# Second FFN up projection, rounds 4 to 11: both units as block products, with weight sums added up in DRAM during the first mixer

## The reference, cut to what matters

```python
h = rms_norm_2(x, ffn_norm_g[l]) * (1 + scale_f) + shift_f
u, v = jnp.split(h @ w_up[l], 2, axis=-1)          # w_up: 1024 x 5632, u and v 2816 columns each
u = causal_depthwise_conv(u, conv_w[l], conv_b[l])
x = x + gate_f * ((jax.nn.silu(u) * v) @ w_down[l])
```

## Time and profile before

| | us |
|---|---|
| runs | 1345.43, 1350.05, 1346.85 |
| median | 1346.85 |
| profiled execution | 1345.38 |
| its span | 1343.4 |
| PE busy | 1331.0 |
| DVE / ACT / POOL busy | 857.3 / 624.0 / 658.7 |
| bytes moved by DMA | 150.59 MB |

### The profile page before, as it was taken

The page is one execution under the profiler, slowest core; times in us unless marked ns, Lnnn a source line. Parts: engine busy times, 40 slices in busy tenths (PEclk is TensorE's granted clock), DMA queues, the critical chain, the costliest instruction groups (busy, mean ns, idle before and its releaser), DMA issues.

```text
span 1343.4 us, 21993 instructions
## 1 busy us (share of the span) xinstructions
PE 1331.0 (99%) x8268; PEld 1135.0 (84%) x8268; DVE 857.3 (64%) x1682; ACT 624.0 (46%) x1097; POOL 658.7 (49%) x369
## 2 busy tenths in 40 slices
PE   8999999999999999999999999999999999999998
PEld 7878888888998888888889976788998999988887
DVE  5898876456778676767897879724579454431222
ACT  7236566564364445453222525675344454542222
POOL 7555232126254444445553489733364776654441
PEclk9999999999999999999999999999999999999999
DMA  7931121115525444444673241121242223252221
GB/s 218 227 102 41 56 63 49 30 35 172 173 87 180 141 142 147 152 149 141 202 228 107 77 112 48 50 64 48 79 157 94 93 96 115 75 201 97 86 87 63
DMA packets 188903, 150.59 MB, mean 112 GB/s; under 512 B 21625, under 2 KB 186723, under 8 KB 188304
## 3 DMA queue, kind: packets, MB, share of 16 engines
q1 hardware_dynamic: 187104, 148.78, 35.8%
q10 hardware_dynamic: 1200, 0.36, 0.1%
q0 software_dynamic: 512, 0.25, 0.1%
HBM read 145.18 MB, written 4.19 MB: 111 GB/s over the span
## 4 chain that ended last, share of the span: by engine, by line
PE 93%; DVE 4%; ACT 1%; issue 1%; POOL 0%; DMA 0%; DVEq 0%; ACTq 0%
PE ps L2638 28%; PE ps L2639 27%; PE ps L2640 27%; PE ps L2832 2%; PE ps L2888 1%; PE ps L2917 1%; DVE qd L2291 1%; DVE hf L2299 1%; PE ps L3120 1%; PE ps L3164 0%; PE ps L3149 0%; PE ps L2722 0%; PE ps L3093 0%; PE ps L3186 0%; DVE hs L2334 0%
## 5 line engine op out<-in xcount | busy, mean ns | idle before, releaser
L914 POOL TENSOR_TENSOR w_lo<-raw,w_hi 128x1024 fp32r<-128x1024 f32 (+2 forms) x210 | 487.2, 2324 | 569.2 <-ACT w_hi L1021 436.0
L2638 PE MATMUL ps<-h_hi,w_hi 128*128 128x512 f32 (+1 forms) x1308 | 478.4, 366 | 0.1
L2639 PE MATMUL ps<-h_lo,w_hi 128*128 128x512 f32 (+1 forms) x1308 | 474.1, 362 | 0.0
L2640 PE MATMUL ps<-h_hi,w_lo 128*128 128x512 f32 (+1 forms) x1308 | 473.5, 362 | 0.0
L2638 PEld LDWEIGHTS ps<-h_hi,w_hi 128*128 128x128 f32 x1308 | 247.2, 189 | 41.9 <-issue 5.0
L2640 PEld LDWEIGHTS ps<-h_hi,w_lo 128*128 128x128 f32 x1308 | 247.1, 189 | 38.7
L1021 ACT ACTIVATE w_hi<-raw 128x1024 fp32r<-128x1024 f32 (+2 forms) x166 | 164.7, 995 | 244.4 <-PE ps L2640 222.9
L2639 PEld LDWEIGHTS ps<-h_lo,w_hi 128*128 128x128 f32 x1308 | 247.4, 189 | 35.6
L2638 PE MATMUL ps<-g_hi,w_hi 128*128 128x512 f32 (+1 forms) x394 | 144.9, 368 | 0.0
L2640 PE MATMUL ps<-g_hi,w_lo 128*128 128x512 f32 (+1 forms) x394 | 144.4, 366 | 0.0
L2639 PE MATMUL ps<-g_lo,w_hi 128*128 128x512 f32 (+1 forms) x394 | 144.3, 366 | 0.0
(11 more groups left out here) (408 smaller groups left out, 1999.2 us busy)
## 6 DMA issues: line engine op xcount, KB each, us to landing
ada<-in_ada_w SPq DMA_DIRECT2D x48, 512.0 KB, 3.7
raw<-in_ffn_w_up SPq DMA_DIRECT2D x22, 1024.0 KB, 4.9
raw<-in_w_up SPq DMA_DIRECT2D x22, 1024.0 KB, 4.9
raw<-in_w_in SPq DMA_DIRECT2D x21, 1024.0 KB, 5.1
raw<-in_ffn_w_down SPq DMA_DIRECT2D x8, 896.0 KB, 5.9
raw<-in_w_down SPq DMA_DIRECT2D x8, 896.0 KB, 5.0
raw<-in_w_in SPq DMA_DIRECT2D x16, 256.0 KB, 3.7
raw<-in_w_out SPq DMA_DIRECT2D x4, 1024.0 KB, 5.1
```

The lines of the kernel that those rows point to most:

```text
L914: pool.tensor_tensor(w_lo[slot % 4][:, 0:nk, :], part[:, :, slot % 2 * P:(slot % 2 + 1) * P], w_hi[slot % 4][:, 0:nk, :].bitcast(F32), ALU ...
L2638: pe.matmul(out_ap, w, x, start=first, stop=False, **kw)
L2639: pe.matmul(out_ap, w, xl, start=False, stop=False, **kw)
L2640: return pe.matmul(out_ap, wl, x, start=False, stop=last, **kw)
```

## The change

**All of rounds 4 to 11 as block products.** `R1` goes from 10 to 11, and both u and v pairs are made in seven products: 16 pairs, numbered p, 112 products in one sequence `PRODUCTS`. For pair p, PE now runs (p,6) (p,2) (p+1,1) (p,7) (p,3) (p+1,5) (p,4); no plain tile stands between. Two sets of four PSUM banks alternate between pairs.

**Work moved between engines.** `w_add` on DVE is gone. Instead DVE makes the low parts of products 2, 3 and 4 (`product_low`), POOL those of 1, 5, 6 and 7. ACT rounds all seven. The second tile of a pair now comes out negated, which the taps and `gated_up` take back.

**Weight sums come from DRAM.** Four tensors `kept_sums1` to `4`, each of shape `[2, 512, 8, 128]` (4 MB), hold the four sums of weight blocks for both kinds. POOL builds them in the first mixer: 16 copies of 1 MB from `w_up_2` (`begin_sum`), 8 adding DMAs of 1 MB in runs of 512 bytes for sums 1 and 3, and 4 adding DMAs of 2 MB in runs of 4 KB for sums 2 and 4, which add sum 1 and sum 2 (`add_to_sum`, `accum_op=ALU.add`). An adding DMA reads its source and its destination and writes the destination. The first add waits for all copies, each add for sum 2 (the first two of 2 MB) for the eight of 1 MB, and each for sum 4 for both of sum 2.

**Loads.** Per pair SP issues six DMAs instead of one: three early (256 KB each: one weight block and sums 1 and 2) into one semaphore, three late (512 KB, and sums 3 and 4 of 256 KB) into another. POOL's descriptor area shrinks from 16 KB to 8 KB a partition, which makes room for two more buffers of sums.

```diff
-R0, R1 = 3, FT // 2 - 1
+R0, R1 = 3, FT // 2
+PRODUCTS = [(0, 1), (0, 5)]
+for _p in range(NPAIR):
+    PRODUCTS += [(_p, 6), (_p, 2)] + [(_p + 1, 1)] * (_p + 1 < NPAIR) + [(_p, 7), (_p, 3)] \
+        + [(_p + 1, 5)] * (_p + 1 < NPAIR) + [(_p, 4)]
+DVE_LOWS = (2, 3, 4)
...
+            def begin_sum(n, kind, rs):
+
+                t, kh = {1: (1, 0), 2: (0, 0), 3: (0, 0), 4: (0, 1)}[n]
+                pool.dma_start(kept_sums[n - 1][kind, :, rs, :], kept_blocks(kind, t, kh)[:, rs, :]).then_inc(sums_kept, 16)
+
+            def add_to_sum(n, kind, ks):
+
+                if n == 1:
+                    pool.wait_ge(sums_kept, SUMS_BEGUN)
+                elif n in (2, 4):
+                    pool.wait_ge(sums_kept, SUMS_BEGUN + 16 * (8 if n == 2 else 10))
+                more = {1: lambda: kept_blocks(kind, 1, 1), 2: lambda: kept_sums[0][kind],
+                        3: lambda: kept_blocks(kind, 1, 0), 4: lambda: kept_sums[1][kind]}[n]()
+                pool.dma_start(kept_sums[n - 1][kind][ks], more[ks], accum_op=ALU.add, max_dma_last_dim=4 * (R1 - R0) * P).then_inc(sums_kept, 16)
...
+            SUM_STEPS = {s: [next(BEGINNINGS) for _ in range(n)] for s, n in
+                         [(s, 1) for s in range(S_K + 1, S_MERGE - 1)] + [(S_MERGE - 1, 3)]
+                         + [(S_MERGE + 3, 2), (S_MERGE + 4, 2), (S_MERGE + 5, 2), (S_MERGE + 6, 1)]}
+            ADDS = [*itertools.product((1, 3), range(2), (slice(0, 2 * P), slice(2 * P, 4 * P))),
+                    *itertools.product((2, 4), range(2), (slice(0, 4 * P),))]
+            ADD_STEPS = dict(zip([S_MERGE + n for n in (7, 8, 9, 11, 12, 13, 14, 15)] + [S_OUT + 2 * n for n in range(4)], ADDS))
...
+            for p in range(NPAIR):
+                n = PAIR_TILE // 2 + p
+                if p < 2:
+                    after_lows(2 * n - 3)
+                else:
+                    sp.wait_ge(lo_done, product_lows(p - 2, 6))
+                for dst, src in LOADS[n]:
+                    sp.dma_start(dst, src).then_inc(raw_in[n % 2], 16)
+                if p >= 2:
+                    after_lows(2 * n - 3)
+                for dst, src in late_blocks(p):
+                    sp.dma_start(dst, src).then_inc(late_in[n % 2], 16)
...
-    nc = bacc.Bacc("TRN2", target_bir_lowering=False, num_devices=1)
+    nc = bacc.Bacc("TRN2", target_bir_lowering=False, num_devices=1, dynamic_dma_scratch_size=8192)
```

More of the change, by code:

```diff
@@ L231, in build @@
         w_lo = [sb(f"w_lo{i}", [P, 8, P], F32R) for i in range(4)]
+        end = (end - 8192) // 32 * 32
+        sums = nc.alloc_sbuf_tensor_at("sums", [P, 2, 2, 4, P], F32, offset=end)
         x_at = offset[0]
@@ L334, in build @@
         g_prod = sb("g_prod", [P, FT, T], at=G0 + 4 * FT * T)
[L335 removed]
+        w_sum = [[hn[:, n, :].rearrange("p (k n) -> p k n", k=4), sums[:, n, 0, :, :], sums[:, n, 1, :, :]] for n in range(2)]
         five = [rstd[:, n * HALF:(n + 1) * HALF] for n in range(2)]
@@ L989, in _ @@
             hgrn_pool(pool, lo)
-            for x in SPLITS[S_UP2 + 4:]:
-                if x in range(S_END):
-                    lo(x)
-                else:
-                    product_lo(*x)
+            for s in range(S_UP2 + 4, PAIR_TILE):
+                lo(s)
+            for p, j in PRODUCTS:
+                if j not in DVE_LOWS:
+                    product_lo(p, j)
+            for s in range(AFTER, S_END):
+                lo(s)
         @block.scalar
@@ L1642, in _ @@
-            hi(up_tile(R1, 1, 1))
-            g_high(R1 - 1, 1)
-            for j in range(4):
-                hi(S_DOWN2 + j)
-                if j < 2:
-                    first_tap(R1, j)
-                else:
-                    silu(R1, j - 2)
-            for t in range(2):
-                g_high(R1, t)
+            copy_one(0)
+            product_hi(7)
+            copy_five(0)
+            product_hi(8)
+            g_high(r, 1)
+            for p in range(NPAIR):
+                r, kind = R0 + p // 2, p % 2
+                last = R0 + (p - 1) // 2
+                q0 = PRODUCT[p, 6] + 7
+                if p and not kind:
+                    g_high(last, 0)
+                if kind:
+                    first_tap(last, 1)
+                if p == NPAIR - 1:
+                    hi(AFTER)
+                product_hi(q0)
+                if kind:
+                    silu(last, 0)
+                product_hi(q0 + 1)
+                if p == NPAIR - 1:
+                    hi(AFTER + 1)
+                if kind:
+                    silu(last, 1)
+                elif p:
+                    g_high(last, 1)
+                product_hi(q0 + 2)
+                if p + 1 < NPAIR:
+                    copy_one(p + 1)
+                    product_hi(q0 + 3)
+                    product_hi(q0 + 4)
+                if not kind:
+                    first_tap(r, 0)
+                if p + 1 < NPAIR:
+                    product_hi(q0 + 5)
+                    copy_five(p + 1)
+                    product_hi(q0 + 6)
```

419 lines of the change are left out of this document (209 added, 210 removed).

## The result

The changed kernel takes **1366.92 us** (median of 4 runs, 1364.22 to 1369.19) against 1347.95 of the kernel before in the same comparison (1345.43 to 1350.05): ratio 1.0141, 95% interval 1.011 to 1.0171. It is slower, as forecast, but by 19.0 us and not by 5, and just above the range.

The account below looks back on a forecast made before the run. PE, busy 99% of the span, was taken as the bound. 1345.4 - 8.3 (fewer columns) + 14 (2 MB adds' stall) = 1351.1, 1352.6 with the offset; forecast 1352 us, range 1339 to 1366.

Parts of the forecast that it names:

- PE's part, -8.3 us: Second FFN's up stage, rounds 4 to 11: 112 products take 161.3 us instead of 169.37, and two extra matmuls go.
- the odd pairs' narrow place: Up stage, v tiles: the seed follows 3.5 to 4.1 us after the u tile, due at 4.3; cost 0, at most 3.5.
- the cost of 0 for xT: After the up stage: xT returns later, but six down tiles of some 5 us precede its first use; cost 0.
- POOL's issues, 1 us each: First mixer: POOL's 28 DMA issues take 1 us each, which its idle time covers.
- Rival (c): First mixer: POOL issues cost 8.3 us a DMA, stalling seven tiles some 5 us each; 1372 us, chance 4%.
- The sixteen copies cost 0: First mixer: 16 MB of copies bring DMA near full, weight loads land some 3 us later, within their lead; cost 0.
- The eight 1 MB adds cost 0: First mixer: each add has 9 us, with 14% of the DMA engines used; cost 0.
- A 2 MB add at twice a copy's time: First mixer's output projection: an add reads source and destination, so takes 11.5 us against 5.75 for a plain copy.
- Rival (a): Output projection: adds run at copy rate, 5.75 us, so the stall is 2 to 4 us; 1338.5 to 1344, chance 30%.
- stands in POOL's queue ahead of tile 55's subtraction: Output projection: the third 2 MB add waits on POOL until the first two land, about 356, delaying that subtraction; +14 us.
- What followed downstream: Before the first mixer's norm: ada load some 12 us late, DVE waits, one PE gap of 7 to 17 us.
- Rival (b): Output projection: adds take 20.4 us, two end at about 375, stall 30 us and more; 1365 to 1375, chance 12%.

Follow-up runs that it names:

- the last run: As all clear, but the last three 1 MB adds behind tiles 37, 41 and 45, not 34 to 36; 1340.49 us, ratio 0.9959.
- all clear: Changed kernel with 2 MB adds behind tiles 146 to 149 (second mixer) and 1 MB adds behind tiles 29 to 36; 1345.7 us, ratio 0.9981.

## Why the prediction was right or wrong

- **PE's part, -8.3 us: right.** 161.27 us for the stage, 8.34 us from norm to end, 8.5 in the run without sums.
- **Nothing else is late in the stage: right,** the odd pairs' narrow place included (no gap over 0.13 us), and so is the cost of 0 for xT.
- **POOL's issues, 1 us each: near, and misleading.** A 1 MB copy took 1.50 us, a 1 MB add 2.1, a 2 MB add 1.0 to 1.4. Rival (c), dear issues, is out by size. But the sum asked only whether POOL has time for them, not whom an issue hits: DVE, up to 3.2 us at a time.
- **The sixteen copies cost 0: right** within what can be told (norm 231.9).
- **The eight 1 MB adds cost 0: wrong.** "9 us each, with 14% of the DMA engines used" compared bandwidth, and 12.6 MB of copies on SP's queue there are indeed free. It left out that an issue can stand until earlier DMAs have landed, with the next tile's or the queries' low parts behind it, and that it holds DVE. It cost 6.3 us in the changed kernel.
- **A 2 MB add at twice a copy's time: right.** An adding 4 KB packet took 327 ns and a copying one 159; 32 packets an engine are 10.5 us, against 11.5 in the sum. Rival (a), copy rate, is out. Half the rate, as in the rule cited with it, is what the records show; whether the two reads are the reason no run tells.
- **The step that failed** is "stands in POOL's queue ahead of tile 55's subtraction", with its +14 us. The term took the adds as a wait on POOL and let the loads beside them share the engines by bytes ("all served" by 359). That landing time was near (360.2, I took 356), but what it does was not: the engines serve turns, not bytes, and a weight load with 1 KB packets got one packet for each 4 KB packet of the adds. It landed after 23.5 us, PE starved for tile 54, POOL came to the third add only at 364.3, when the first two were done, and the stall was 21.1 us, of which some 5 are the lower clock after the waits. The run with the first two adds alone has no third add to stand at and still loses 13.3 us. That 14 and 21.1 us are of like size is luck, since the path was another.
- **What followed downstream was right in part:** DVE waited for conditioning loads (15.1 and 11.6 us), and PE had one large wait before the norm (11.9). The load that the sum followed was issued at 368.13, 21 us later than before and not 12. But the first of DVE's waits was for a load issued at 345.04, ahead of the third add, which itself starved beside the first two.
- **A slip in the sum:** the slack behind DVE's last squares is 368.03 - 366.68 = 1.35 us by its own rows, not 1.2. Nothing hangs on it.
- **The sum:** 1352 + 6.3 (1 MB adds) + 7.1 (21.1 instead of 14) = 1365.4. The remaining 1.5 us are the offset from profiled run to median, 2.7 us here against the 1.5 assumed, and rounding.
- **Rival (b)** (1365 to 1375) has the measured time in it, but its mechanism, 20 us an add with two landed at about 375, did not occur: they had landed at 360.2.

## What to carry to other kernels

A background DMA is not priced by its bytes alone. Ask what it does to the load beside it in turns of packets: a load with small packets beside large adding ones lives on one packet a turn, and how far loads run ahead decides how many such DMAs in a row are free (here one, not two). And an issue on POOL is an instruction that can stand for older DMAs and that, together with a subtraction right behind it, can hold a DVE instruction beside it, so its place is chosen by what DVE and the rest of POOL's queue do there. The changed kernel and the last run differ only in where POOL issues the adds; the same change gives 1.4% more time or 0.4% less.

## What the hardware showed that I had not expected

- While both queues had work, POOL's and SP's got equal numbers of packets whatever their size: 541 and 537 of 4 KB and 1 KB, 689 and 688 of 1 KB each.
- A load that SP issued beside a 2 MB add moved its first packet after 3.6 to 3.7 us, and after 1.0 us in the kernel before.
- Adding packets on POOL's queue: 65 ns for 512 B, 101 for 1 KB, 327 for 4 KB; plain ones 27, 46 and 159. So an add costs about 2.1 to 2.4 times a copy at each size.
- Four DVE instructions beside POOL's issue of a 1 MB add took 3.3 to 4.2 us where the same ones took 0.55 to 0.97 without it, and ended with the POOL subtraction behind the issue, 1.6 to 2.5 us after the issue. Not every issue meets one: three of the eight in "all clear" held a DVE instruction (one of them for 0.8 us only), and none in the last run.
- POOL stood at an issue of 2048 runs until an earlier DMA had landed: 12 to 13 us with 2 MB adds in 1 KB runs, up to 9.5 with 1 MB adds in 512 B runs. With 2 MB in 4 KB runs two adds could be under way at once, 5.4 us apart; but the fourth stood 9.46 us in the changed kernel until the third had landed, with no wait for it in the program. Why the one and not the other stays open.
- A wait of PE of 2.50 us in the attention was followed by matmuls at half clock, one of 1.75 us was not; the 6.3 us lost there are 4.3 of waits and 2 of that.
